# A float32 decoder of six layers on one core: the token transform from half-width tables, and a reordered begin

## What is computed

```
mkv = mem @ w_mem_kv                              # memory keys and values, once
h = layer_norm(x, ln_in_g, ln_in_b)
for each layer of kind "a":
    proj = h @ w_in_a[j]                          # gates and memory queries
    branch = fourier_mix(h)
    y = concat([branch, memory_attention(qm, mk, mv)]) * silu(gate)
    h = layer_norm(DEEPNORM_ALPHA * h + y @ w_out[i], ...)

def fourier_mix(h):                               # 4 groups of 256 channels
    hg = h.reshape(B, S, FNET_GROUPS, D // FNET_GROUPS)
    return jnp.fft.fftn(hg, axes=(1, 3), norm="ortho").real.reshape(B, S, D)
```

## Time and profile before

| | |
|---|---|
| Runs | 1345.26 us median of 3 (1341.03 to 1345.51) |
| The profiled execution | 1344.37 us, of it 1342.6 us in the span |
| TensorE busy | 1270.0 us (95%) |
| VectorE busy | 864.9 us (64%) |
| ScalarE busy | 701.7 us (52%) |
| DMA | 197.53 MB, 147 GB/s on average |

### The profile page before, as it was taken

The page is one execution under the profiler, slowest core; times in us unless marked ns, Lnnn a source line. Parts: engine busy times, 40 slices in busy tenths (PEclk is TensorE's granted clock), DMA queues, the critical chain, the costliest instruction groups (busy, mean ns, idle before and its releaser), DMA issues.

```text
span 1342.6 us, 19912 instructions
## 1 busy us (share of the span) xinstructions
PE 1270.0 (95%) x7972; PEld 1110.9 (83%) x7972; DVE 864.9 (64%) x1518; ACT 701.7 (52%) x1015; POOL 2.4 (0%) x8
## 2 busy tenths in 40 slices
PE   5999999999999999998998998999999997999997
PEld 5997777778888787887887986989898986989895
DVE  5646996586564756548456886665546887665645
ACT  3624477453457566565525675544443676544442
POOL 0000000000000000000000000000000000000000
PEclk8999999999999999999998998999999999999998
DMA  9325432445543335233333443456564543456560
GB/s 299 116 78 188 157 111 79 157 137 200 181 155 121 126 118 166 85 126 102 126 119 113 154 138 100 151 185 211 167 216 118 157 144 112 148 180 219 163 223 40
DMA packets 146913, 197.53 MB, mean 147 GB/s; under 512 B 4716, under 2 KB 102278, under 8 KB 146694
## 3 DMA queue, kind: packets, MB, share of 16 engines
q1 hardware_dynamic: 146694, 196.22, 45.5%
q0 software_dynamic: 128, 0.04, 0.0%
HBM read 195.20 MB, written 1.05 MB: 146 GB/s over the span
## 4 chain that ended last, share of the span: by engine, by line
PE 77%; DVE 13%; ACT 5%; issue 4%; DMA 1%; SPq 0%; DVEq 0%; ACTq 0%
PE bank L461 21%; PE bank L462 21%; PE bank L463 21%; PE bank L547 4%; DVE w_lo L2079 4%; DVE stat L2099 2%; PE bank L749 2%; PE bank L1036 1%; PE bank L1073 1%; ACT w_hi L1542 1%; DVE arena L2093 1%; PE bank L660 1%; PE bank L898 1%; DMA arena<-in_mem 1%; DVE stat L2096 1%
## 5 line engine op out<-in xcount | busy, mean ns | idle before, releaser
L2079 DVE TENSOR_TENSOR w_lo<-w_raw,w_hi 128x2048 fp32r<-128x2048 f32 (+5 forms) x190 | 413.3, 2183 | 131.6 <-ACT w_hi L1542 129.3
L1542 ACT ACTIVATE w_hi<-w_raw 128x2048 fp32r<-128x2048 f32 (+5 forms) x190 | 346.1, 1828 | 284.8 <-PE bank L463 274.2
L461 PE MATMUL bank<-h_hi,w_hi 128*128 128x256 f32 x976 | 279.7, 287 | 5.3 <-DVE w_lo L2079 2.1
L462 PE MATMUL bank<-h_lo,w_hi 128*128 128x256 f32 x976 | 276.1, 283 | 0.0
L463 PE MATMUL bank<-h_hi,w_lo 128*128 128x256 f32 x976 | 276.0, 283 | 0.0
L461 PE MATMUL bank<-w_hi,r_hi 128*128 128x512 f32 (+3 forms) x536 | 208.4, 389 | 5.0 <-DVE r_lo L2753 4.2
L462 PE MATMUL bank<-w_lo,r_hi 128*128 128x512 f32 (+3 forms) x536 | 205.0, 382 | 0.0
L463 PE MATMUL bank<-w_hi,r_lo 128*128 128x512 f32 (+3 forms) x536 | 204.9, 382 | 0.0
L461 PEld LDWEIGHTS bank<-h_hi,w_hi 128*128 128x128 f32 x976 | 187.0, 192 | 12.1 <-issue 7.6
L462 PEld LDWEIGHTS bank<-h_lo,w_hi 128*128 128x128 f32 x976 | 187.1, 192 | 0.6
L463 PEld LDWEIGHTS bank<-h_hi,w_lo 128*128 128x128 f32 x976 | 187.1, 192 | 0.0
(11 more groups left out here) (283 smaller groups left out, 1370.5 us busy)
## 6 DMA issues: line engine op xcount, KB each, us to landing
w_raw<-in_mlp_w SPq DMA_DIRECT2D x64, 1024.0 KB, 5.4
w_raw<-in_w_out SPq DMA_DIRECT2D x24, 1024.0 KB, 5.1
w_raw<-in_w_in_c SPq DMA_DIRECT2D x48, 512.0 KB, 4.6
w_raw<-in_w_in_c SPq DMA_DIRECT2D x18, 1024.0 KB, 5.1
w_raw<-in_w_in_a SPq DMA_DIRECT2D x12, 1024.0 KB, 5.9
w_raw<-in_w_in_b SPq DMA_DIRECT2D x12, 1024.0 KB, 5.2
w_raw<-in_w_in SPq DMA_DIRECT2D x8, 1024.0 KB, 5.2
w_raw<-in_w_out SPq DMA_DIRECT2D x8, 512.0 KB, 3.8
```

The costliest lines, as they stand in the source:

```text
L461: nc.tensor.matmul(o, lhs[0], rhs[0], start=start, stop=False)
L462: nc.tensor.matmul(o, lhs[0], rhs[1], start=False, stop=False)
L1542: nc.scalar.activation(w_hi[:, u % SPLIT_SLOTS, 0:kts * n], w_raw[:, u % RAW_SLOTS, 0:kts * n], ACT.Copy).then_inc(w_rounded.sem, w_rounde ...
L2079: v.tensor_tensor(w_lo[:, s, 0:m], w_raw[:, u % RAW_SLOTS, 0:m], w_hi[:, s, 0:m].bitcast(F32), ALU.subtract)\
```

## The change

**Token transform.** A cosine over the 256 tokens is the same at a token and at its mirror (256 minus it), and a sine only changes its sign. The table is now made for the 2 tokens that are their own mirror and one token of each of the 127 pairs: 129 columns of cosines and 127 of sines. `tokens(t)` still has 8 products, of 129 or 127 columns, and cosine and sine sums now stay apart in the bank. ScalarE copies the sine sums out (`sines`, 254 numbers in a row), and VectorE's new `gated_tokens` puts cosine plus sine at a token and cosine minus sine at its mirror: one copy and six additions or subtractions, and then the product with the gate and the split.

**Begin.** The memory rows are loaded ahead of unit 0, x in 4 pieces of 64 partitions, and the part of the tables that layer b0 and later ones use is loaded after unit 6. TensorE multiplies the identity by itself 14 times ahead of the memory transposes, and by 512 columns of the memory rows 6 times behind them, into a bank that nobody reads. `mem v` now comes ahead of the transposes of the normalised rows. ScalarE rounds unit 0 behind the memory rows, and reads `mem k` and `mem v` earlier; VectorE splits unit 1 between the statistics of the second half and its `row_norm`.

```diff
+MIRRORED = ((1, 8, 9, 16), (16, 40, 40, 64), (64, 160, 160, 256))
+SELF_MIRROR = (0, 8)
+N_COS = S // 2 + 1
+N_SIN = S // 2 - 1
...
-    a = 2 * np.pi * np.outer(t, t) / S
-    put("dft_tok", np.concatenate([np.cos(a), -np.sin(a), np.sin(a)], 1) / 16)
+    pairs = [p for p0, p1, _, _ in MIRRORED for p in range(p0, p1)]
+    assert all((t[p0 + i] + t[m1 - 1 - i]) % S == 0 for p0, p1, _, m1 in MIRRORED for i in range(p1 - p0))
+    a = 2 * np.pi * np.outer(t, t[list(SELF_MIRROR) + pairs]) / S
+    sines = np.sin(a[:, len(SELF_MIRROR):])
+    put("dft_tok", np.concatenate([np.cos(a), -sines, sines], 1) / 16)
...
+    put("decay_room", np.zeros((P, CONST_AT["dft_tok"][0] + NB * SSD_H * P - sum(x.shape[1] for x in parts))))
...
+        def sine_sums(t):
+            at = t % 2 * 256
+            return split_t[:, 1, at:at + 2 * N_SIN].rearrange("p (c s) -> p c s", c=2)
...
             pe.wait_ge(ident_loaded, 16)
+            for _ in range(14):
+                nc.tensor.matmul(bank[3][:, 0:P], ident, ident, start=True, stop=True)
             pe.wait_ge(mem_loaded, 16)
...
+            for _ in range(6):
+                nc.tensor.matmul(bank[3][:, :], ident, mem_in[:, 0, 0:512], start=True, stop=True)
             for j in range(4):
                 pe.wait_ge(r_ready.sem, r_ready.at(("mem", "t", j)))
             feature_major(("mem", "k"), 4, rows_of(A["w_mem_kv"], 0, KT, 0, MEM_W), rT)
-            hidden_from_rows("in", 0)
...
             unit_done[u] = ("mem", "v")
+            hidden_from_rows("in", 0)
...
-                        dt = K("dft_tok").rearrange("p (b s c) -> p b s c", b=NB, s=3)
+                        dt = K("dft_tok").rearrange("p (b c) -> p b c", b=NB)
+                        tables = [[dt[:, b, 0:N_COS], dt[:, b, N_COS:S], dt[:, b, S:S + N_SIN]] for b in range(NB)]
...
                             for part in range(2):
+                                c0, c1 = ((0, N_COS), (N_COS, S))[part]
                                 for b in range(NB):
-                                    i = nc.tensor.matmul(o[:, c * S:(c + 1) * S], spectra[:, b, t, c, part, :], dt[:, b, part if c == 0 else 2 * part, :], start=part + b == 0, stop=part + b == 2)
+                                    i = nc.tensor.matmul(o[:, c * S + c0:c * S + c1], spectra[:, b, t, c, part, :], tables[b][part if c == 0 else 2 * part], start=b == 0, stop=b == 1)
                         i.then_inc(product_done.sem, product_done.next((L, "f2", t)))
...
             sp.dma_start(const[:, 0:P], A["const"][:, 0:P]).then_inc(ident_loaded, 16)
+            sp.dma_start(mem_in, A["mem"][0].rearrange("(b p) d -> p b d", p=P)).then_inc(mem_loaded, 16)
             load_unit(0)
-            sp.dma_start(mem_in, A["mem"][0].rearrange("(b p) d -> p b d", p=P)).then_inc(mem_loaded, 16)
             xv = A["x"][0].rearrange("(c b a) d -> a b c d", a=4, b=4)
             for a in range(4):
-                for b in range(4):
-                    p0 = (a % 2) * 64 + b * 16
-                    sp.dma_start(x_in[p0:p0 + 16, a // 2, :], xv[a, b]).then_inc(x_loaded, 16)
+                p0 = (a % 2) * 64
+                sp.dma_start(x_in[p0:p0 + 64, a // 2, :], xv[a]).then_inc(x_loaded, 16)
             load_unit(1)
             load_unit(2)
             sp.dma_start(const_once, A["const"][:, n_kept:]).then_inc(consts_loaded, 16)
-            sp.dma_start(const[:, P:], A["const"][:, P:n_kept]).then_inc(consts_loaded, 16)
+            late = CONST_AT["axial_cos"][0]
+            sp.dma_start(const[:, P:late], A["const"][:, P:late]).then_inc(consts_loaded, 16)
 
             at = 0
...
+                if u == 2 * RAW_SLOTS:
+                    sp.dma_start(const[:, late:], A["const"][:, late:n_kept]).then_inc(tables_loaded, 16)
...
-            round_unit(0)
             for j in range(4):
                 act.wait_ge(product_done.sem, product_done.at(("mem", "t", j)))
                 nc.scalar.activation(flat2(r_hi[:, 2 * j:2 * j + 2, :]), bank[4 + j][:, :], ACT.Copy).then_inc(split_hi.sem, split_hi.next(("mem", j)))
+            round_unit(0)
+            evac(("cols", "a"), col_a[:], bank[0][:, 0:N_COL_A], ahead=0)
             round_unit(1)
-            evac(("cols", "a"), col_a[:], bank[0][:, 0:N_COL_A])
-            act.wait_ge(x_loaded, 256)
+            act.wait_ge(x_loaded, 64)
             for b, n in BY_SCALAR:
+                if b == 1:
+                    round_unit(2)
                 act.wait_ge(row_stats.sem, row_stats.at(("in", b)))
                 nc.scalar.activation(z[:, b, n * 512:(n + 1) * 512], x_in[:, b, n * 512:(n + 1) * 512], ACT.Identity,
                                      scale=S_(8 + b, 1), bias=S_(10 + b, 1)).then_inc(rows_normal.sem, rows_normal.next(("in", b, n)))
+            evac(("mem", "k"), flat2(mkT[:, :, :]), bank[4][:, :], ahead=0)
+            evac(("mem", "v"), flat2(mv[:, :, :]), bank[5][:, :], ahead=0)
             hidden_hi("in", "a0", split_t, tiles_read)
             act.wait_ge(ident_loaded, 16)
             act.wait_ge(consts_loaded, 32)
             nc.scalar.activation(flat2(dft_hi[:, :, :]), const_once, ACT.Copy)
             nc.scalar.activation(ident_r[:], ident, ACT.Copy).then_inc(tables_rounded.sem, tables_rounded.next(0))
-            evac(("mem", "k"), flat2(mkT[:, :, :]), bank[4][:, :])
-            evac(("mem", "v"), flat2(mv[:, :, :]), bank[5][:, :])
+            round_weights(("a0", "qm"), 1)
...
+                    def sines(t):
+                        round_weights((L, "f2", t))
+                        act.wait_ge(product_done.sem, product_done.at((L, "f2", t)))
+                        if t >= 2:
+                            act.wait_ge(out_read.sem, out_read.at((L, "f2", t - 2)))
+                        sums = bank[A_SPECTRUM_BANK[t]][:, :].rearrange("p (c s) -> p c s", c=2)
+                        nc.scalar.activation(sine_sums(t), sums[:, :, N_COS:S], ACT.Copy).then_inc(sines_read.sem, sines_read.next((L, "f2", t)))
...
                     pair_exp(0)
                     pair_exp(1)
+                    sines(0)
                     gate_silu(0)
                     pair_turned(0)
+                    sines(1)
                     pair_turned(1)
-                    for u in range(1, 4):
+                    gate_silu(1)
+                    for u in (2, 3):
+                        sines(u)
                         gate_silu(u)
                 elif kind == "b":
...
+            def gated_tokens(L, j, key, src):
+
+                t = split_t[:, 0, :]
+                both, sums = [a.rearrange("p (c s) -> p c s", c=2) for a in (t, src)]
+                pair = slice(2 * j, 2 * j + 2)
+                product(key, 1)
+                sines = sine_sums(j)
+                dve.wait_ge(sines_read.sem, sines_read.at(key))
+                at, step = len(SELF_MIRROR), SELF_MIRROR[1] - SELF_MIRROR[0]
+                v.tensor_copy(both[:, :, 0:2 * step:step], sums[:, :, 0:at])
+                for p0, p1, m0, m1 in MIRRORED:
+                    n, of = p1 - p0, at - len(SELF_MIRROR)
+                    v.tensor_tensor(both[:, :, p0:p1], sums[:, :, at:at + n], sines[:, :, of:of + n], ADD)
+                    ins = v.tensor_tensor(both[:, :, m1 - 1:m0 - 1:-1], sums[:, :, at:at + n], sines[:, :, of:of + n], SUB)
+                    at += n
+                ins.then_inc(out_read.sem, out_read.next(key))
+                dve.wait_ge(out_read.sem, out_read.made)
+                stt(t, t, 1.0 / ALPHA, flat2(gate[:, pair, :]), MUL, MUL)
+                gated(L, j, key, src, (1, 2))
+
...
-            dve.wait_ge(x_loaded, 256)
+            dve.wait_ge(x_loaded, 64)
             for b in range(NB):
                 for n in range(2):
                     link(v.bn_stats(S_(128 + 12 * b + 6 * n, 6), x_in[:, b, n * 512:(n + 1) * 512]))
+                if b == 1:
+                    weights(("mem", "v"), 0)
                 row_norm("in", b)
             normal_half("in", x_in[:, 1, 0:512])
-            weights(("mem", "v"), 0)
+            weights(("a0", "qm"), 0)
             dve.wait_ge(act_read.sem, act_read.at(("cols", "a")))
...
-                        key, n_b = ((L, "mo"), B_OUT_BANK) if of == 4 else ((L, "f2", of), A_SPECTRUM_BANK[of])
+                        key = (L, "mo") if of == 4 else (L, "f2", of)
                         weights(key)
                         dve.wait_ge(gate_read.sem, gate_read.at((L, "gate", of)))
-                        gated(L, of, key, bank[n_b][:, :], ahead=1)
+                        if of == 4:
+                            gated(L, of, key, bank[B_OUT_BANK][:, :], ahead=1)
+                        else:
+                            gated_tokens(L, of, key, bank[A_SPECTRUM_BANK[of]][:, :])
```

More of the change, by code:

```diff
@@ L239, in build @@
         spectrum_read = Steps("spectrum_read")
+        sines_read = Steps("sines_read")
         row_recip = Steps("row_recip")
@@ L262, in build @@
         consts_loaded = ctx.enter_context(nc.semaphore("consts_loaded"))
```

(11 more changed lines are left out.)

## The result

The changed kernel takes 1351.75 us (median of 6 runs, 1349.69 to 1357.04), the kernel before 1343.86 us in the same comparison (6 runs, 1340.47 to 1345.51). The ratio is 1.0071, interval 1.0052 to 1.0089: slower by 0.7%, where 1339.4 was forecast, and outside the range. The profiled execution took 1357.04 us (span 1355.2), 12.67 more than the one of before (1344.37).

What follows compares the result with a forecast made beforehand. VectorE was taken to bound the begin until gate 4 at 40.84 us, mostly TensorE layer a0. 1344.37 - 6.1 (two a layers) + 0.2 (begin) = 1338.5 us, for the median 1339.4; range 1333.5 to 1346.5.

Steps and rivals of the forecast that it cites:

- the sum from W to `gate 4`: Begin, unit 0 split until gate 4 starts: 25.2 us with the new order, 22.8 before, so gate 4 at 41.0.
- W: Begin: the time when unit 0 is split, 15.8 us forecast (bounds 14.9 and 17.0), 18.03 in the kernel before.
- The sentence on unit 1: Begin: unit 1, landed at 18.28 and rounded at 20.2 before, is wanted at 20.7, so it holds nothing up.
- The begin: Start of the kernel to gate 4: 2.2 us gained in W, lost by the new order; 0.2 us given away.
- the fillers: Begin, TensorE: 14 identity products ahead of the memory transposes, forecast to end at 7.6 to 8.9 us.
- Tokens: Layers a, TensorE's token calls: each 1.73 us shorter; tokens 0 save 0, tokens 1 0.8, tokens 2 and 3 3.46.
- Layer a1 has the same instructions in the same order: Second a layer: taken to behave as a0, so the same 3.06 us saving was counted for it.
- Layer a0 saves 3.06: First a layer: 4.26 us saved on TensorE less 1.2 for longer gated_tokens on VectorE (bounds 2.4 and 3.3).
- The clock falls in the new holes: Rival, 6%: TensorE's clock falls behind all four new idle times, 13.6 us in all, giving 1353, slower by 0.6%.
- The row of 806.83: Profile row of the kernel before, cited against the clock falling: a hole of 2.77 us left the clock at 1.00.
- The sum: Whole kernel: 1344.37 less 6.1 for two layers plus 0.2 for the begin, 1338.5 us; 1339.4 for the median.
- the 0.9: Whole kernel: the profiled execution lies 0.9 us under the median of the runs, so the median forecast is 1339.4.

Runs made afterwards that it cites:

- its twin without fillers: The changed kernel with x in 16 transfers and both loops of identity products (14 and 6) left out: 1341.71 us, against 1341.81 with them.

## Why the prediction was wrong

The step that failed is the start of the sum from W to `gate 4`: "Now the order is: statistics of both halves and one `row_norm`". It lets the statistics of x start as soon as unit 0 is split, at 15.8, and takes x as landed by then. The edit that joins 16 transfers to 4 was given no price at all, and the landing of x had no term in the sum. The trace has unit 0 split at 15.21 and x landed at 25.69, a wait of 10.48 us on the chain. `mem v` lost some 1.5 us more, since it came behind TensorE's idle 11.64 us at a lower granted clock (7.4 us from its first product to the transposes, 5.9 with x in 16 transfers). So `gate 4` came at 52.76 in place of 41.0. The runs show this edit alone to cost 7.9 us on the kernel before.

The sentence on unit 1, "Unit 1 has the same bytes ahead of it in the queue as before", was wrong in the same way: the bytes are the same, the engines that carry them aren't, and it landed at 28.40 in place of 18.28. But with x so late it was rounded in time.

With this edit undone the rest of the working can be held against the trace:

- *The begin.* W: 15.8 said, 15.70 measured. `mem v`: 22.9 said, 22.91 measured. `gate 4`: 41.0 said, 41.17 measured. In the changed kernel W was 15.2 and the fillers ended at 7.6; both were right, and neither mattered.
- *Tokens.* Holes of 2.3 said, 2.19 measured in a0 and 2.77 to 2.78 in a1. "Layer a1 has the same instructions in the same order" is not so: there f1 stands ahead of `qm` and `gate 4`, and the hole ahead of scores 1 was 1.10 already, not 0.5; tokens 1 saved 0.8 said, 0.75 measured (from the transposes of pair 0 to values 0 3.67 us in place of 4.42). `gated_tokens` longer by 1.2 said, 1.11 measured (copy at 106.58, the gate's product at 107.69). The output product waits 1.51 for `w_lo`, 1.5 said. Layer a0 saves 3.06 said, 2.97 measured.
- *The clock.* "The clock falls in the new holes" had 6% and all four holes or none. One of them, in a1, did it in four of six profiles, and cost 2.7 to 2.9 us in two of them, about the whole gain of that layer, and 1.4 to 1.5 in the other two. The row of 806.83, where a hole of 2.77 us left the clock alone, was taken as a rule, and it is one case.
- *The sum.* It adds 0.9 us, since the profiled execution of the kernel before lay that far under a median of 3 runs. In larger sets of runs (17 to 23) that median is 1344.2 to 1344.6, as the profiled execution, so the 0.9 was chance; without it the forecast would be 1338.5, further from what came. The forecast saving is 5.9 us. The kernel with x in 16 transfers saves 2.7 in the median (1344.52 to 1341.81). Falls of the clock in a1 would be of the size of what is missing, but its own profile and that of its twin without fillers, the fastest execution of each, show none, and the slower executions have no profile: why it falls short stays open.

## What to carry to other kernels

Joining DMA transfers can cost time though the bytes stay: look at the outermost dimension of the source and the destination as the instruction carries them, and where it is small (4 and 2 here), count the engines. A low DMA share beside a pending landing is what it looks like in a profile, and what was queued behind (unit 1 here) was late as well. A saving on TensorE ahead of a wait only widens a hole: tokens 0 saved nothing, and the hole that it left was followed by losses of 1.4 to 2.9 us in four profiles. Repeating work that is there already filled it at no price here. When an engine's work grows on the path (`gated_tokens`), look for what stands behind it and has its inputs: here the split of unit 9 fitted into an idle time of 3.2 us just ahead.

## What the hardware showed that wasn't expected

- The rate of a queue that is down to one kind of transfer is a multiple of 25 to 26 GB/s: 52 with an outermost 2, 100 to 102 with an outermost 4.
- SP's own issue stopped for 15.1 us in a transfer of 258 KB while four DMA engines were behind. It went on at 25.84, when x had landed (25.69). In the kernel before with x in 4 transfers the same issue took 15.16 us and ended at 25.36, with x landed at 25.20; with consecutive rows it took 8.02 and ended at 14.30, before 3.90. So it isn't only the transfers on four engines that hold it. That a full queue does is the reading that fits; no run tests it.
- Executions of one kernel spread with the granted clock: 10.2 us between a mean of 0.993 and of 0.984, more than the 7.9 us that this whole change moved.
